# Streaming stage of a decoder step: scores in four quarters of the array, a third bank for transposes, a new order for the block choice

## The chip, the cores and the metric

One core of one Trainium2 chip runs the whole program as one launch. The metric is the device time of one execution in microseconds. Three executions of the kernel before were timed; the median counts.

## The reference, cut to what matters

One inference step of a decoder layer: 512 prompt tokens and 8 sequences with one new token each share the weights (width 1024, float32). The change lies in the attention of the 8 sequences. Each has 8 query heads of 64 in 2 groups, 1024 cached positions and a memory of 256 rows, and four kinds of scores against its own keys:

```python
# per sequence b, head h; one query token each
s_c = q @ kc.T          # 63 compressed blocks: kc = gelu(rows(32 tokens) @ w1) @ w2 + ...
imp = sum_heads(softmax(s_c)) for 17 blocks of 64 tokens; 16 are kept (the first and the last two always)
s_s = q @ k_sel.T       # 1024 cached keys and the new one, only in the chosen blocks
s_w = q @ k_win.T       # a window: 511 cached keys and the new one
s_m = qm @ k_mem.T      # 4 memory heads over 256 rows
o = g0 * softmax(s_c) @ vc + g1 * softmax(s_s) @ v_sel + g2 * softmax(s_w) @ v_win ;  o_mem = softmax(s_m) @ v_mem
```

Keys lie in memory by rows and must be turned (transposed on TensorE) before they can be multiplied.

## The kernel before

The program has stages: projection and streaming in one block (to about 305 us), then the prompt's attention and mixing, the routing, and 32 experts whose weights stream from memory up to the end. Each stage starts behind a barrier of all engines. The change touches only `stream()`.

**Streaming.** `ORDER` is 0, 1, 8, 2, 3, ..., 7; 8 stands for the prompt (its compression alone). A sequence comes in two halves of 512 cached rows. SyncE loads half i into one of four landing slots (`load_half`, L542; its waits are in `half_free`, L626: half i - 4 sorted, its values copied, its selection keys turned). GpSimd copies the compression rows of a half into one of two sorted buffers (`take_kv`, L803) and the selection values away (`take_vs`, L809). TensorE turns a sequence in 8 units of four 128 x 128 transposes (`turn`, L922): units 0 to 3 are compression rows (L933), 4 and 5 selection keys straight from the landing slot (L937), 6 window keys (L941), 7 memory keys (L945). Unit 4 is thus the one that frees a sequence's first half for the load of the half four further on. Units alternate between PSUM banks 4 and 5; ScalarE copies the even ones out (L871), VectorE the odd ones (L659). A unit waits until the copy of the unit two before is done (L926).

**Scores** (`score`, L979) of the sequence before are put between the first units of the next, in four parts: part 0 is the selection keys' first half and the window keys, 512 columns each with 64 stationary columns, one in the array's lower half (bank 0, partitions 0 to 63), one in the upper (bank 2, partitions 64 to 127); part 1 the selection keys' second half (bank 1); part 2 the memory keys (two products of 256 columns, 32 stationary columns, bank 3); part 3 the new keys (two of one column). `Q` holds 64 columns for each sequence, of which only its own 8 are not zero, so all sequences add up in the same 64 partitions.

**Compression** (`compress`, L958): 16 taps each for keys and values follow each three entries of `ORDER`, so the sequences come in three groups: (0, 1, prompt), (2, 3, 4), (5, 6, 7). Between the taps and their second product stands gelu, on VectorE (L666 to L673) with a tanh on ScalarE (L878); gelu stands in both engines' lists ahead of the copies of the next sequences.

**The end.** After the last keys' taps: VectorE copies the memory scores out of PSUM and takes their maximum, the same for the window, `keep_k(2)`, then the compressed scores (L741); ScalarE takes the exponents of memory, window, compressed (L894, L897, L900). TensorE sums the heads' probabilities (L1049, "the choice's product"), VectorE finds the block that falls out (L750 to L756), adds the mask while copying the selection scores out of PSUM (L761), takes the maximum over 1025 columns (L707), ScalarE the exponents (L903), then VectorE scales the window's and the choice's weights (L716). TensorE transposes the window's, memory's and compressed weights (L1054 to L1058), waits, transposes the choice's (L1065), and does all value products (L1074 to L1095) with 8 stationary columns in four quarters of the array. The last taps of the values' compression are spread over the waits. The output rows are gathered last (L1107).

## Time and profile before

| what | us |
|---|---|
| median of 3 runs | 1017.05 |
| runs | 1017.04 to 1019.19 |
| the profiled execution's own time | 1020.41 |
| its span, first to last instruction | 1018.6 |
| TensorE busy | 896.5 (88%) |
| VectorE, ScalarE, GpSimd busy | 315.2, 195.0, 124.2 |

In the rows further down, PE is TensorE, PEld its weight loads, DVE VectorE, ACT ScalarE, POOL GpSimd, SPq SyncE's queue. A row of a timeline is a run of equal instructions: start, duration until the end of the last, engine, line, operation, what it writes and reads, shape and count; in brackets the idle time of the engine before it and who ended it. A float32 product of the scores counts as two records. Ends of matmuls are modelled, so for TensorE the distance from start to start says more than a duration. PEclk is the clock that was granted to TensorE, as a share of 2.4 GHz.

### The profile page before, as it was taken

The numbers are of one execution on the slowest core, as the hardware profiler recorded it, in microseconds if no ns is written. First come the engines' busy times: TensorE is split into PE (matmuls) and PEld (weight loads), VectorE is DVE, ScalarE is ACT, GpSimd is POOL, SyncE is SP. The second block draws the span as 40 slices with busy tenths as digits, with TensorE's granted clock in tenths as the row PEclk, the third lists the DMA queues.
The fourth block names the chain that finished last, engine by engine and source line by source line (L and its number), as shares of the span: only waits on it lengthen the run. The fifth ranks groups of instructions, "written<-read, shape, count | busy, mean of one in ns | idle before, by whom it ended". The sixth has DMA issues, their size and how long they took to land.

```text
span 1018.6 us, 13659 instructions
## 1 busy us (share of the span) xinstructions
PE 896.5 (88%) x5483; PEld 500.1 (49%) x5483; DVE 315.2 (31%) x685; ACT 195.0 (19%) x468; POOL 124.2 (12%) x143
## 2 busy tenths in 40 slices
PE   7999989998988889989998999889788787787887
PEld 3445445564554446656555555445443444344443
DVE  3162242313335786564552111111111111111110
ACT  1031121202115675561110000001000000000000
POOL 0010023212000011120001111111111111111001
PEclk9999999999988899999997999999999999999999
DMA  9773127677208000005978999999999999999996
GB/s 363 322 237 102 57 75 172 137 174 180 90 2 299 1 1 2 1 1 216 384 291 320 416 415 415 411 417 413 412 420 415 410 417 408 416 412 414 416 410 224
DMA packets 66472, 272.12 MB, mean 267 GB/s; under 512 B 12048, under 2 KB 28367, under 8 KB 40991
## 3 DMA queue, kind: packets, MB, share of 16 engines
q1 hardware_dynamic: 52359, 254.17, 63.9%
q0 software_dynamic: 7376, 12.85, 4.6%
q10 hardware_dynamic: 6672, 4.20, 1.8%
q8 instruction: 45, 0.74, 0.3%
q14 instruction: 20, 0.16, 0.1%
HBM read 264.63 MB, written 19.10 MB: 279 GB/s over the span
## 4 chain that ended last, share of the span: by engine, by line
DMA 24%; PE 24%; SPq 12%; DVE 3%; ACT 3%; issue 3%; POOL 1%; POOLq 0%; DVEq 0%; ACTq 0%
DMA room<-in_w_gate 9%; SPq L2200 9%; PE ps L2340 6%; SPq L2204 4%; DMA spare<-in_w_up 3%; DMA w_b<-in_w_up 3%; PE ps L1905 3%; DMA room<-in_w_up 3%; DMA w_b<-in_w_down 3%; PE ps L1479 3%; DMA w_a<-in_w_up 3%; PE ps L2367 2%; PE ps L1387 1%; ACT w_a L1732 1%; PE ps L1405 1%
## 5 line engine op out<-in xcount | busy, mean ns | idle before, releaser
L2340 PE MATMUL ps<-room 128*64 128x256 f32 x800 | 98.2, 394 | 30.3 <-DMA room<-in_w_up 17.9
L2340 PEld LDWEIGHTS ps<-room 128*64 128x64 f32 x800 | 57.3, 140 | 67.4 <-DMA room<-in_w_up 26.0
L2254 POOL DMA_INDIRECT out_y<-room,halves x32 | 50.1, 1565 | 279.9 <-ACT room L2520 276.3
L2340 PE MATMUL ps<-w_a,room 128*64 128x256 f32 x576 | 69.3, 390 | 16.6 <-DMA w_a<-in_w_up 8.8
L2340 PE MATMUL ps<-w_b,room 128*64 128x256 f32 x576 | 67.7, 383 | 16.1 <-DMA w_b<-in_w_up 9.7
L505 PE MATMUL ps<-w_b,room 128*128 128x454 f32 x192 | 75.3, 544 | 1.0 <-ACT w_a L437 1.0
L2520 ACT ACTIVATE room<-ps,slot_w 128x512 f32<-128x512 f32 x32 | 22.0, 687 | 277.6 <-PE ps L2367 273.3
L972 PE MATMUL ps<-room,w_a 128*128 128x378 f32 x192 | 62.5, 483 | 0.0
L2340 PEld LDWEIGHTS ps<-w_a,room 128*64 128x64 f32 x576 | 40.9, 139 | 42.4 <-DMA w_a<-in_w_up 13.3
L2431 DVE SCALAR_TENSOR_TENSOR room<-room,ps 128x256 f32<-128x256 f32 x32 | 13.5, 422 | 152.3 <-ACT room L2514 152.3
L2340 PEld LDWEIGHTS ps<-w_b,room 128*64 128x64 f32 x576 | 40.0, 137 | 41.1 <-DMA w_b<-in_w_up 15.3
L2433 DVE TENSOR_TENSOR room<-room,ps 128x256 f32<-128x256 f32 x32 | 13.5, 421 | 133.7 <-PE ps L2340 133.7
L505 PEld LDWEIGHTS ps<-w_b,room 128*128 128x128 f32 x192 | 36.2, 190 | 37.4 <-issue 37.4
L2367 PE MATMUL ps<-room,consts 128*64 128x512 f32 x208 | 47.8, 599 | 0.5 <-DVE consts L2437 0.5
L972 PEld LDWEIGHTS ps<-room,w_a 128*128 128x128 f32 x192 | 36.0, 190 | 22.8
L2437 DVE COPY consts<-ps 128x256 f32<-128x256 f32 x32 | 13.6, 425 | 107.4 <-PE ps L2324 107.4
L2514 ACT ACTIVATE room<-ps 128x256 f32<-128x256 f32 x32 | 12.3, 383 | 170.8 <-PE ps L2340 170.8
L1732 ACT ACTIVATE w_a<-ps,room 128x256 f32<-128x256 f32 (+3 forms) x80 | 40.2, 514 | 12.7 <-DVE room L1579 12.6
L2208 POOL DMA_INDIRECT xg<-hn_dram,pairs x16 | 16.9, 1059 | 200.7 <-PE ps L2354 130.7
L659 DVE COPY room<-ps 128x512 f32<-128x512 f32 x33 | 22.8, 691 | 52.5 <-PE ps L933 39.9
L1479 PE MATMUL ps<-w_b,room 128*128 128x256 f32 x128 | 31.4, 401 | 3.5 <-POOL room L1339 2.0
L2367 PE MATMUL ps<-w_b,consts 128*64 128x512 f32 x144 | 33.1, 599 | 0.7 <-DMA w_b<-in_w_down 0.7
(376 smaller groups left out, 1221.0 us busy)
## 6 DMA issues: line engine op xcount, KB each, us to landing
room<-in_w_down SPq DMA_DIRECT2D x26, 1024.0 KB, 28.1
room<-in_w_gate SPq DMA_DIRECT2D x25, 1024.0 KB, 28.4
room<-in_w_up SPq DMA_DIRECT2D x25, 1024.0 KB, 28.3
w_a<-in_w_gate SPq DMA_DIRECT2D x18, 1024.0 KB, 27.0
w_a<-in_w_up SPq DMA_DIRECT2D x18, 1024.0 KB, 27.9
w_a<-in_w_down SPq DMA_DIRECT2D x18, 1024.0 KB, 28.4
w_b<-in_w_gate SPq DMA_DIRECT2D x18, 1024.0 KB, 28.3
w_b<-in_w_up SPq DMA_DIRECT2D x18, 1024.0 KB, 27.6
```

The lines of the kernel that those rows point to most:

```text
L505: ins = nc.tensor.matmul(in_psum(t, a), turned_rows(t)[:, k, 0:r], rhs, start=(k == 0), stop=(k == KD - 1))
L659: nc.vector.tensor_copy(dst, src).then_inc(out_d, 1)
L972: ins = nc.tensor.matmul(ps[:, 6 + q, 0:NG3], w1[:, q, l, :], XT[q][:, :, :, l % 8, l // 8:l // 8 + NC_S].rearrange("p s g m -> p (s g) m" ...
L1479: ins = nc.tensor.matmul(ps[:, 7, half:2 * half], mT[:, k, t * P:t * P + P], self.w_out[:, k, half * c:half * c + half], start=(k == 0), s ...
L1732: ins = nc.scalar.activation(pr[:, i // n, i % n, :], sc[:, i // n, i % n, :], ACT.Exp, bias=stt[:, u % 6, 0, i:i + 1], scale=-1.0, accum_ ...
L1905: ins = nc.tensor.matmul(ps[0:r, b + a, :], m[:, k, :], w_out[:, k, 512 * a:512 * a + 512], start=(k == 0), stop=(k == KD - 1))
L2200: sp.dma_start(self.gate_or_up(u, j), src[:, 4 * j:4 * j + 4, :]).then_inc(self.unit_in[j][u % RING], 16)
L2204: sp.dma_start(self.down_half(u, j), src[:, j, :, :]).then_inc(self.unit_in[j][u % RING], 16)
L2254: pool.indirect_dma_start(out=rows, out_offset=bass.IndirectOffsetOnAxis(ap=self.halves[:, n:n + 1].bitcast(U32), axis=0), in_=yb[:, slot, ...
L2340: ins = nc.tensor.matmul(ps[h * CAP:h * CAP + CAP, bank, 0:FH], xT[:, n // 2 % 2, k, CAP * slot:CAP * slot + CAP], w[k // 4][:, k % 4, h * ...
L2367: ins = nc.tensor.matmul(ps[a * CAP:a * CAP + CAP, 6 + n % 2, :], hT[:, j, h * CAP:h * CAP + CAP], wd[h][:, j, 512 * a:512 * a + 512], sta ...
L2520: nc.scalar.activation(yb[:, n % 2, :], ps[0:2 * CAP, 6 + n % 2, :], ACT.Copy, scale=self.slot_w[:, n:n + 1]).then_inc(y_copied, 1)
```

## The change

- Scores: a sequence's products are cut to the 32 columns that hold its own 8, and its four score sets go to four quarters of one bank: selection keys' halves to partitions 0 to 31 and 32 to 63, window keys to 64 to 95, memory keys to 96 to 127. Sequences 0 to 3 use bank 0, 4 to 7 bank 1. All five products are issued together, behind unit 1 of the next sequence; the new keys' part stays behind unit 3.
- Bank 2 is free for it: from the ninth unit on, turns go round banks 4, 5, 2, and wait for the copy of the unit three before.
- ScalarE copies the window's and the selection's scores from the quarters to 64 partitions in SBUF (six copies); VectorE copies only the memory's and the small ones.
- The choice: VectorE takes each block's maximum over the unmasked scores beforehand (16 numbers a row), adds the mask to these 16 and takes the maximum over 17, instead of over 1025; the mask's addition works in SBUF. `keep_k(2)` moves behind the window's maximum. The window's weights are scaled ahead of the choice.
- The compressed scores use two quarters. The choice's product comes after three more taps instead of four.
- TensorE does the window's value products ahead of the choice's transposes, which it did after them before.

```diff
+        win_taken, sel_taken = S("win_taken"), S("sel_taken")
...
-        sel0, win0, misc, hid, cmp_ = ps[:, 0:2, :], ps[:, 2, :], ps[:, 3, :], ps[:, 6, :], ps[:, 7, :]
+        win0, misc, hid, cmp_ = ps[:, 2, :], ps[:, 3, :], ps[:, 6, :], ps[:, 7, :]
...
         place = {s: j for j, s in enumerate(ORDER)}
...
+        early = units[ORDER[0]]
+        bank_of = [4 + n % 2 if n < early else (4, 5, 2)[(n - early) % 3] for n in range(NUNIT)]
+        earlier = [max((m for m in range(n) if bank_of[m] == bank_of[n]), default=None) for n in range(NUNIT)]
...
+        tops = late[0:64, 4000:4017]
...
                 for u in range(1, units[s], 2):
...
+                    src = ps[:, bank_of[first[s] + u], :]
...
-                        src = ps[:, 5, :].rearrange("p (g m r) -> p g r m", g=G, r=8)
+                        src = src.rearrange("p (g m r) -> p g r m", g=G, r=8)
...
-                        src = ps[:, 5, :]
...
-            ch.then(nc.vector.tensor_copy(smb[:, :], misc[64:96, 128:384]))
+            ch.then(nc.vector.tensor_copy(smb[:, :], ps[96:128, 0, 0:MEM]))
             peak(1, 32, smb[:, :], "mmax")
...
-            nc.vector.tensor_copy(swb[:, 1:512], win0[64:128, 1:512])
+            nc.vector.tensor_copy(ssb[:, 1024:1025], misc[0:64, 64:65])
...
+            dve.wait_ge(win_taken, 2)
+            peak(2, 64, swb[:, 1:513], "wmax")
             keep_k(2)
-            peak(2, 64, swb[:, 1:513], "wmax")
-            dve.wait_ge(cs_in_psum, 1)
+            dve.wait_ge(sel_taken, 4)
+            ch.then(nc.vector.tensor_reduce(tops[:, 0:2 * PAST // PAGE].rearrange("p (c k) -> p c k", c=4),
+                                            ssb[:, 0:PAST].rearrange("p (c t k j) -> p c k t j", c=4, t=2, k=4), AX.XY, ALU.max))
+            dve.wait_ge(cs_in_psum, 2)
...
             weights(0, 64, scb[:, 0:NC_S], None, "pc")
...
+            weights(2, 64, swb[:, 1:513], g64[:, 2:3], None)
+            ch.then(nc.vector.tensor_scalar(dgn[:, 1, :], self.c(C_ID, 64, 64), swb[:, 512:513], None, ALU.mult))
+            marks["wp"] = ch.n
             dve.wait_ge(imp_in_psum, 1)
...
+            ch.then(nc.vector.tensor_tensor(tops[:, 0:16], tops[:, 0:16], imp[:, 2, :], ALU.add))
+            nc.vector.tensor_copy(tops[:, 16:17], ssb[:, 1024:1025])
...
-                out4 = ssb[:, 0:1024].rearrange("p (c t k j) -> p c t k j", c=4, t=2, k=4)
-                in4 = sel0[0:64, :, :].rearrange("p a (c t k j) -> p (a c) t k j", c=2, t=2, k=4)
+                out4 = ssb[:, 0:1024].rearrange("p (c t k j) -> p c t k j", c=4, t=2, k=4)[:, :, par, :, :]
...
-                nc.vector.tensor_tensor(out4[:, :, par, :, :], in4[:, :, par, :, :], mask, ALU.add)
-            ch.then(nc.vector.tensor_copy(ssb[:, 1024:1025], misc[0:64, 64:65]))
-            peak(3, 64, ssb[:, 0:1025], "smax")
...
-            dve.wait_ge(es, 2)
-            weights(2, 64, swb[:, 1:513], g64[:, 2:3], None)
-            ch.then(nc.vector.tensor_scalar(dgn[:, 1, :], self.c(C_ID, 64, 64), swb[:, 512:513], None, ALU.mult))
-            marks["wp"] = ch.n
+                ins = nc.vector.tensor_tensor(out4, out4, mask, ALU.add)
+            ch.then(ins)
+            peak(3, 64, tops[:, 0:17], "smax")
...
                 for u in range(0, units[s], 2):
...
+                    src = ps[:, bank_of[first[s] + u], :]
...
-                        src = ps[:, 4, :].rearrange("p (g m r) -> p g r m", g=G, r=8)
+                        src = src.rearrange("p (g m r) -> p g r m", g=G, r=8)
...
-                        dst, src = KsT[:, 0:512] if u == 4 else KwT[:, :], ps[:, 4, :]
+                        dst = KsT[:, 0:512] if u == 4 else KwT[:, :]
...
             tanh(2, 0)
+            act.wait_ge(scored, NB)
+            for g in range(2):
+                nc.scalar.copy(swb[32 * g:32 * g + 32, 1:512], ps[64:96, g, 1:512]).then_inc(win_taken, 1)
             act.wait_ge(steps_d, marks["mmax"])
...
+            for g in range(2):
+                for hf in range(2):
+                    nc.scalar.copy(ssb[32 * g:32 * g + 32, 512 * hf:512 * hf + 512], ps[32 * hf:32 * hf + 32, g, :]).then_inc(sel_taken, 1)
             act.wait_ge(steps_d, marks["wmax"])
...
             def turn(s, u):
...
-                if n >= 2:
-                    pe.wait_ge(out_d if n % 2 else out_a, n // 2)
-                dst = ps[:, 4 + n % 2, :]
+                if earlier[n] is not None:
+                    pe.wait_ge(out_d if earlier[n] % 2 else out_a, earlier[n] // 2 + 1)
+                dst = ps[:, bank_of[n], :]
...
             def score(s, part):
-                q = Q[:, 64 * s:64 * s + 64]
-                if part == 0:
+                g = s // 4
+                q = Q[:, 64 * s + 32 * g:64 * s + 32 * g + 32]
+                if part == 1:
...
-                    nc.tensor.matmul(sel0[0:64, 0, :], q, KsT[:, 0:512], **add)
-                    nc.tensor.matmul(win0[64:128, :], q, KwT[:, :], **add)
-                elif part == 1:
-                    nc.tensor.matmul(sel0[0:64, 1, :], q, KsT[:, 512:1024], **add)
-                elif part == 2:
+                    nc.tensor.matmul(ps[0:32, g, :], q, KsT[:, 0:512], **add)
+                    nc.tensor.matmul(ps[32:64, g, :], q, KsT[:, 512:1024], **add)
+                    nc.tensor.matmul(ps[64:96, g, :], q, KwT[:, :], **add)
...
-                        nc.tensor.matmul(misc[64:96, 128:384], Qm[:, a, 32 * s:32 * s + 32], KmT[:, a, :], **add)
-                else:
+                        nc.tensor.matmul(ps[96:128, 0, 0:MEM], Qm[:, a, 32 * s:32 * s + 32], KmT[:, a, :], **add)
+                elif part == 3:
...
-                        ins = nc.tensor.matmul(misc[0:64, 64 + a:65 + a], q, kTn[:, a, s:s + 1], **add)
+                        ins = nc.tensor.matmul(misc[32 * g:32 * g + 32, 64 + a:65 + a], q, kTn[:, a, s:s + 1], **add)
...
                         score(before, u)
...
-                    score(before, 2)
...
-                    for a in range(4):
+                    for a in (0, 1, 3):
...
             compress(2, 0, range(16))
-            for part in range(4):
-                score(NB - 1, part)
+            score(NB - 1, 1)
+            score(NB - 1, 3)
...
             compress(2, 1, range(4, 6))
...
-            for b in range(NB):
-                ins = nc.tensor.matmul(misc[0:64, 0:NC_S], Q[:, 64 * b:64 * b + 64], kcT[:, place[b], 0:NC_S], start=False, stop=False, skip_group_check=True)
-            ins.then_inc(cs_in_psum, 1)
-            compress(2, 1, range(6, 10))
+            for i in range(4):
+                for g in range(2):
+                    b = 4 * g + i
+                    ins = nc.tensor.matmul(misc[32 * g:32 * g + 32, 0:NC_S], Q[:, 64 * b + 32 * g:64 * b + 32 * g + 32], kcT[:, place[b], 0:NC_S], **add)
+                    if i == 3:
+                        ins.then_inc(cs_in_psum, 1)
+            compress(2, 1, range(6, 9))
...
-            compress(2, 1, range(10, 16))
...
-            pe.wait_ge(steps_d, marks["wp"])
+            compress(2, 1, range(9, 16))
...
+            pe.wait_ge(steps_d, marks["cg"])
...
             pe.wait_ge(zeroed, 7)
             nc.tensor.matmul(win0, zb2[0:1, 0:128], zb2[0:1, :], start=True, stop=False, skip_group_check=True)
+            pe.wait_ge(sel_taken, 4)
...
-            pe.wait_ge(steps_d, marks["sp"])
-            for j in range(8):
-                nc.tensor.transpose(ps[:, 4, 64 * j:64 * j + 64], ssb[:, 128 * j:128 * j + 128], ident(64))
-            nc.tensor.matmul(hid[0:NB, 256:320], self.c(C_S8, NB, 64), dgn[:, 0, :], start=True, stop=True).then_inc(pT_in_psum, 1)
...
+            pe.wait_ge(steps_d, marks["sp"])
+            for j in range(8):
+                nc.tensor.transpose(ps[:, 4, 64 * j:64 * j + 64], ssb[:, 128 * j:128 * j + 128], ident(64))
+            nc.tensor.matmul(hid[0:NB, 256:320], self.c(C_S8, NB, 64), dgn[:, 0, :], start=True, stop=True).then_inc(pT_in_psum, 1)
```

## Rows read from the trace of the kernel before

**Rows 1.** Busy time by stage: us, length, busy of each engine (x instructions), PEclk, DMA share, GB/s.
```profile
139.00:163.00 24.00, 19.79 (x112) 11.52 (x110) 11.11 (x34) 7.61 (x14) 13.37 (x26) 0.93 0.62 151
...
183.50:208.00 24.50, 22.48 (x141) 13.56 (x140) 11.07 (x19) 7.27 (x13) 6.85 (x12) 1.00 0.82 184
...
228.30:257.20 28.90, 25.90 (x156) 14.66 (x155) 10.91 (x18) 7.30 (x13) 6.91 (x12) 1.00 0.66 167
...
287.40:294.20 6.80, 6.80 (x108) 3.74 (x106) 1.69 (x4) 1.20 (x3) 0.00 (x0) 0.51 0.01 2
```

**Rows 2.** TensorE in order of time, sequence 5: start us, us, engine line op, xcount.
```profile
228.87 0.64 PE L987 MATMUL ps<-room 128*64 128x512 f32 x1
...
229.88 0.66 PE L933 MATMUL ps<-consts,xg 128*128 128x128 f32 x4
230.47 1.07 PE L990 MATMUL ps<-room 128*64 128x512 f32 x2
...
232.05 1.05 PE L993 MATMUL ps<-room 128*32 128x256 f32 x4
...
233.62 0.39 PE L996 MATMUL ps<-room 128*64 128x1 f32 x4
233.94 1.19 PE L937 MATMUL ps<-consts,w_a 128*128 128x128 f32 x8
235.27 0.66 PE L941 MATMUL ps<-consts,room 128*128 128x128 f32 x4
```

**Rows 3.** GpSimd in order of time, copies out of the landing buffer.
```profile
201.79 1.17 POOL L803 COPY xg<-w_a 128x512 f32<-128x512 f32 x2 [2.75 <-DMA w_a<-in_cache_kv]
...
246.40 1.17 POOL L803 COPY xg<-w_a 128x512 f32<-128x512 f32 x2 [10.85 <-DMA w_a<-in_cache_kv]
...
250.95 1.17 POOL L803 COPY xg<-w_a 128x512 f32<-128x512 f32 x2 [2.82 <-DMA w_a<-in_cache_kv]
```

**Rows 4.** TensorE in order of time, first transposes of late half-sequences.
```profile
203.10 0.63 PE L933 MATMUL ps<-consts,xg 128*128 128x128 f32 x4 [0.39 <-POOL xg L803]
...
252.27 0.63 PE L933 MATMUL ps<-consts,xg 128*128 128x128 f32 x4 [1.32 <-POOL xg L803]
```

**Rows 5.** All engines in order of time, 267 to 287 us.
```profile
270.31 0.55 DVE L673 SCALAR_TENSOR_TENSOR room<-spare,room 128x378 f32<-128x378 f32 x1 [0.58 <-ACT spare L878]
...
277.17 0.35 ACT L900 ACTIVATE room<-room 64x63 f32<-64x63 f32 x1 [1.05 <-DVE room L708]
...
279.06 0.33 PE L1049 MATMUL ps<-room,consts 64*64 64x64 f32 x2
...
280.96 1.28 DVE L761 TENSOR_TENSOR w_a<-ps,room 64x512 f32<-64x512 f32 x2
...
283.77 1.15 ACT L903 ACTIVATE w_a<-w_a,room 64x1025 f32<-64x1025 f32 x1 [6.16 <-DVE room L708]
...
286.45 0.71 PE L1065 MATMUL ps<-consts,w_a 64*128 64x64 f32 x8
```

**Rows 6.** TensorE in order of time, products with the values in quarters.
```profile
291.64 3.12 PE L1080 MATMUL ps<-w_a 128*4 128x256 f32 x32
...
295.23 1.93 PE L1088 MATMUL ps<-w_b,w_a 128*8 128x128 f32 x64
```

**Rows 7.** Groups by line, 139 to 305 us: xcount, busy us, mean ns, idle before.
```profile
L659 DVE COPY room<-ps 128x512 f32<-128x512 f32 x33 | 22.8, 691 | 52.5 <-PE ps L933 39.9 <-PE ps L937 6.5 <-PE ps L945 6.1
...
L871 ACT COPY room<-ps 128x512 f32<-128x512 f32 x33 | 19.2, 583 | 57.4 <-PE ps L933 37.4 <-PE ps L937 13.4 <-PE ps L941 6.5
```

**Rows 8.** All engines in order of time, 239 to 240 us.
```profile
239.84 0.57 ACT L871 COPY room<-ps 128x512 f32<-128x512 f32 x1
```

**Rows 9.** TensorE in order of time, the first group of sequences.
```profile
144.06 2.11 PE L937 MATMUL ps<-consts,w_a 128*128 128x128 f32 x8
...
153.23 0.63 PE L933 MATMUL ps<-consts,xg 128*128 128x128 f32 x4 [0.50 <-POOL xg L803]
...
163.08 20.27 PE L972 MATMUL ps<-room,w_a 128*128 128x378 f32 x63
```

## The prediction

> **What bounds the kernel now.** I first read the busy time by stage [rows 1]. The change touches one stage, the streaming of the eight cached sequences, from about 139 to 305 us. In its three groups of sequences (139 to 163, 183.5 to 208 and 228.3 to 257.2 us) TensorE is busy for 19.8 of 24, 22.5 of 24.5 and 25.9 of 28.9 us; between the groups it runs the compression taps, which the change leaves alone. Every other engine is busy for under 60% of any group. So TensorE's list of work sets the pace, with gaps. The DMA share of 0.82 and 0.66 says that the loads come close behind.
>
> Then the list itself [rows 2]. In sequence 5 a unit of four transposes takes 0.59 us when nothing holds it (229.88 to 230.47). Between the first four units stand the scores of the sequence before: 1.01 us (228.87 to 229.88, two products of 512 columns side by side in halves), 1.00 (one in a half), 0.99 (memory keys), and 0.32 (new keys, 233.62 to 233.94): 3.3 us. Two units in a row take 1.33 us instead of 1.18: with two banks a unit waits for the copy of the one two before.
>
> Third, the loads [rows 3]: GpSimd takes sequence 7's two halves at 246.40 and 250.95 only because they landed then (10.85 and 2.82 us of idle before), and sequence 4's second at 201.79. TensorE waits for these copies [rows 4]: 0.39 us at 203.10, 1.32 us at 252.27. These two places matter most: a faster TensorE arrives early there.
>
> Last, the end of the stage [rows 5]: the gelu of the last compression ends at 270.86; the exponents of the compressed scores start at 277.17, the block choice's product at 279.06, the mask's two additions (1.28 us) at 280.96, the choice's exponents (1.15 us) at 283.77, their transposes at 286.45. From there TensorE works to the end of the stage nearly without a gap. The next stage starts behind a barrier, so what the stage gains should pass on whole. Later stages are not changed.
>
> **The scores in quarters.** Five products (three of 512 columns, two of 256 into one quarter) replace those that took 3.0 us; the 0.32 us part stays. Do four quarters overlap? Value products do it already [rows 6]: 32 products of 128 columns in 1.93 us are 60 ns each, where half a score of 512 columns alone takes 1.0 us, or 250 ns per 128. That is four at once. The 256-column ones (16 in 3.12 us, mostly at half clock [rows 1]) agree. None has 512 columns, so I bound the set by 1.0 (perfect) and 2.0 us (pairs only) and take 1.1, nearest to those rows. Gain: 1.9 us for each score on the path.
>
> **The third bank.** A unit then waits for the copy of three before. A copy takes 0.691 us on VectorE and 0.583 on ScalarE [rows 7], each engine taking every second unit (1.18 us apart), so this hides: 0.15 us saved per pair, some 0.3 to 0.35 per sequence. It doesn't hide where gelu lies ahead of the copies: ScalarE's copy of sequence 6's first unit begins at 239.84 [rows 8], 3.3 us after the last unit of sequence 5. With units 0 to 2 and a score in 2.9 us, unit 3 then waits about 1 us. The load hides that in groups 2 and 3.
>
> **Group 1** [rows 9]. Sequence 1's second half comes from GpSimd at about 153.1 us (TensorE's unit at 153.23), held by the gate's chain and not by TensorE. The score ahead of it costs nothing either way. Behind it the 0.99 us part and the bank waits go: sequence 1 ends 1.2 us earlier. The next score (before the taps at 163.08) saves 1.9 and two bank or copy waits 0.4. Sum 3.5 us.
>
> **Group 2.** Sequence 4's load starts when sequence 2's fifth unit is turned. No score lies ahead of it there, so relative to the group's start that comes only 0.3 us earlier. DMA carries this load at its rate (share 0.82 over the group [rows 1]), so its second half is ready at 202.96 less 0.3. What lies behind shrinks from 4.9 us (203.10 to 208.0) to six units, the 0.32 and nothing else: 3.6. Gain 0.3 + 1.3 = 1.6 us, while TensorE alone would have offered 4.8 (two scores and three sequences' bank waits): it now waits some 2.6 us before this half.
>
> **Group 3.** Here the score of sequence 4 lies ahead of the fifth unit: the load starts 1.8 us earlier. Behind its second half again 4.9 becomes 3.6 (252.27 to 257.2). Gain 3.1 us. The waits before the two halves of sequence 7 grow to some 2.6 and 2.2 us.
>
> Sum by the last compression's taps: 3.5 + 1.6 + 3.1 = 8.2 us.
>
> **The end of the stage** [rows 5], counted from the end of those taps (267.4 before). The last score is 1.9 us shorter, but VectorE starts on the softmaxes only once the gelu is done, at +3.5 in both kernels: nothing. ScalarE gets six copies more. Two (window) run while VectorE does the gelu's last step and cost nothing: without that cover 1.2 us. The memory exponents start at +4.5 and end at +5.2, then four copies at 0.58 [rows 7] until +7.5; VectorE waits for them with the compressed scores queued behind, then takes the blocks' maxima (1024 columns, like the two additions of 1.28 us): +8.9. Compressed exponents at +9.5 against +9.8 (277.17). Their normalisation takes 1.0, so the choice's product starts at +10.5. Before, it stood at +11.7 behind four taps; now three taps and shorter compressed scores leave TensorE free at +9, with 1.5 us of wait. From that product to the choice's exponents it was 4.7 us. The window's weights (1.0 us) come ahead of it, 0.65 of them uncovered; the 1.2 us maximum over 1025 columns becomes 17 columns (0.17). Sum 4.35: exponents at +14.85 against +16.35. Meanwhile TensorE does the remaining seven taps, the window's transposes and the zeroing (to +17.0), waits for ScalarE's copies behind the exponents, and starts the value products at +17.4. Before, the equal amount of work started at +19.05 (286.45). Gain 1.6 us.
>
> **Sum and clock.** 8.2 + 1.6 = 9.8 us. Against this stands TensorE's clock. The granted clock was 0.51, the 1.2 GHz level, from 287.4 to 294.2 us [rows 1], behind a wait and small products; and two units that take 1.19 us took 2.11 at 144.06 [rows 9] behind a wait of 2.7 us for ScalarE. The change makes three or four waits of that size. A stretch at half clock costs up to half its length where TensorE is the bound (3.4 us for 6.8), and nothing where it waits. I bound it by 0 and 5 us and take 1.7. The stretch near the end may also vanish, which would give up to 3.4 back. Forecast: 8.1 us off.
>
> The profiled execution took 1020.41 us for a span of 1018.6; so the sum gives 1012.3 for it. The runs' median is 1017.05; by the same difference 1008.9, which I give as 1009.0.
>
> **Rivals.** (a) *The copies become the bound.* If each unit waits for a copy (0.69 + 0.1 us) instead of taking 0.59, six units behind each late half and in group 1 take 1.2 us more: 9.8 - 3.6 - 1.7 = 4.5 us off, 1012.5. Against it: each copying engine is busy under half of a group [rows 1]. The Trainium skill (TensorEngine Tiling (Array Packing), section Performance Considerations) says that after a fourfold speedup the copying out of PSUM may become the bottleneck; by that rule the result would be this one. Chance 0.08.
> (b) *Slower: the clock.* Place: the waits before sequences 4's and 7's halves, in group 1, and before the choice's product. If each of the four is followed by 6.8 us at half clock under dense taps, that is 4 x 3.4 = 13.6 us against 9.8: 1017.05 + 3.8 = 1020.9. It decides once more than 19.6 us at half clock fall on bound work. For it: the two stretches above. Against: most of such a stretch would fall on the wait itself, and taps before and after are dense. The Trainium skill (TensorE: Matmul & The Clock Gate, section HAM oscillation) describes this: waits for DMA between bursts make each burst start cold. By that rule the time would lie towards this rival. Chance 0.03; a partial form (5 us off, 1012) 0.12.
> (c) *Quarters overlap only in pairs*: 0.9 us more for the three scores on the path: 5.4 us off, 1011.7. The value products speak against it. Chance 0.06.
> (d) *The half-clock stretch at the end goes*: 11.5 us off, 1005.5. Chance 0.1.
> (e) *The loads follow TensorE less or more than I think* (something other than the fifth unit starts them): at worst groups 2 and 3 gain only the 1.3 each behind the half: 3.5 + 2.6 + 1.6 less 1.7 is 6.0 us off, 1011.0. Chance 0.06.
> The rest, 0.55, is the forecast.
>
> **How the numbers follow.** Outside 1004.5 to 1013.0 lie (b) in full, parts of (d) and of the partial clock case: under 2 in 10. A measurement of this kernel can tell about 0.2% (2 us) from no change. Faster by more: 0.95. Within: 0.02. Slower: 0.03.
>
> **What would show it.** A sequence's five score products in about 1.1 us; units 0.59 us apart; GpSimd's copies of sequence 7's halves still waiting for DMA, with TensorE waiting over 2 us for each; taps starting 3.5, 5.1 and 8.2 us earlier; the choice's exponents about 15 us after the last compression's taps of the first kind. The forecast is wrong if TensorE doesn't wait for GpSimd at sequence 7 (then more is gained), if ScalarE's four copies end later than 7.5 us after those taps, or if half-clock stretches grow by over 5 us.

## The result, and the profile after

| what | kernel before | changed kernel |
|---|---|---|
| median, us | 1019.27 (10 runs, 1017.04 to 1024.91) | 1011.04 (10 runs, 1008.01 to 1013.75) |
| the profiled execution's own time, its span | 1020.41, 1018.6 | 1012.05, 1010.2 |
| TensorE busy | 896.5 | 874.9 |

The ratio is 0.9907, with a 95% interval of 0.988 to 0.9933: the changed kernel is faster, by 8.2 us between the medians, which is under 1%. The forecast was a gain of 8.1 us, to 1009.0. The changed kernel's median lies 2.0 us above that because the kernel before came out 2.2 us higher over ten runs than over the three that the forecast started from. So the size of the gain was right, but in part by luck: in this pair of traces the edits were worth some 12.5 us where 9.8 were forecast, and the clock cost some 4.2 us where 1.7 were taken (worked out below).

First the busy time by stage, as in [rows 1], of the changed kernel: the three groups of sequences, 14 us of the end, and the stretch that had half the clock in group 3.

```profile
139.90:158.80 18.90, 13.01 (x113) 9.68 (x111) 11.32 (x34) 7.65 (x14) 9.60 (x19) 1.00 0.58 152
179.20:204.20 25.00, 17.93 (x142) 14.83 (x141) 11.07 (x19) 7.04 (x13) 8.58 (x15) 0.86 0.87 202
224.50:249.00 24.50, 18.68 (x156) 14.34 (x155) 10.91 (x18) 7.12 (x13) 6.91 (x12) 0.93 0.78 192
241.30:244.50 3.20, 2.97 (x17) 2.12 (x18) 0.69 (x1) 0.59 (x1) 0.64 (x2) 0.50 1.15 269
278.00:292.00 14.00, 12.13 (x302) 9.51 (x290) 3.12 (x6) 2.04 (x5) 0.00 (x0) 1.00 0.01 2
```

The reader is to see that TensorE's busy time fell in each group (19.8, 22.5 and 25.9 before), that groups 1 and 3 are shorter and group 2 is not, and that its clock was granted in full at the end, where before it was 0.51 for 6.8 us.

Then TensorE's list in sequence 5, which answers to [rows 2]. The numbers behind the columns are those of the rows before.

```profile
225.44 0.62 PE L1005 MATMUL ps<-room 128*32 128x512 f32 x1
225.44 0.62 PE L1006 MATMUL ps<-room 128*32 128x512 f32 x1
225.45 0.62 PE L1007 MATMUL ps<-room 128*32 128x512 f32 x1
225.46 0.62 PE L1009 MATMUL ps<-room 128*32 128x256 f32 x2
225.89 0.59 PE L1005 MATMUL ps<-room 128*32 128x512 f32 x1
...
226.44 1.09 PE L950 MATMUL ps<-consts,xg 128*128 128x128 f32 x8
227.46 0.29 PE L1012 MATMUL ps<-room 128*32 128x1 f32 x4
227.68 1.09 PE L954 MATMUL ps<-consts,w_a 128*128 128x128 f32 x8
228.60 0.60 PE L958 MATMUL ps<-consts,room 128*128 128x128 f32 x4
229.04 0.62 PE L962 MATMUL ps<-consts,room 128*128 128x128 f32 x4
```

All four quarters begin their first pass within 0.02 us and their second 0.45 us later; the next unit follows 1.00 us after the first. And a unit now takes 0.44 to 0.46 us from start to start (227.68 to 228.60 for two, then 229.04), where the forecast had 0.59.

Third, TensorE's waits for GpSimd's copies of the late halves, in TensorE's own list, answering to [rows 4], with what comes behind them:

```profile
192.72 1.06 PE L950 MATMUL ps<-consts,xg 128*128 128x128 f32 x8 [1.40 <-POOL xg L813]
...
198.93 1.94 PE L950 MATMUL ps<-consts,xg 128*128 128x128 f32 x8 [4.15 <-POOL xg L813]
...
201.10 1.97 PE L954 MATMUL ps<-consts,w_a 128*128 128x128 f32 x8
...
204.15 20.49 PE L989 MATMUL ps<-room,w_a 128*128 128x378 f32 x64
...
241.53 1.94 PE L950 MATMUL ps<-consts,xg 128*128 128x128 f32 x8 [3.71 <-POOL xg L813]
...
245.85 1.06 PE L950 MATMUL ps<-consts,xg 128*128 128x128 f32 x8 [0.79 <-POOL xg L813]
```

and the copies themselves in GpSimd's list, answering to [rows 3]:

```profile
191.40 1.17 POOL L813 COPY xg<-w_a 128x512 f32<-128x512 f32 x2 [7.69 <-DMA w_a<-in_cache_kv]
...
197.61 1.17 POOL L813 COPY xg<-w_a 128x512 f32<-128x512 f32 x2 [4.48 <-DMA w_a<-in_cache_kv]
...
240.22 1.17 POOL L813 COPY xg<-w_a 128x512 f32<-128x512 f32 x2 [10.83 <-DMA w_a<-in_cache_kv]
...
244.53 1.17 POOL L813 COPY xg<-w_a 128x512 f32<-128x512 f32 x2 [2.59 <-DMA w_a<-in_cache_kv]
```

TensorE's waits in groups 2 and 3 for these copies were 1.7 us in all at the two places of [rows 4], and 2.4 with the 0.67 us ahead of sequence 7's first half; at four places they are 10.05 now. Sequence 4's halves land 6.2 us apart (4.5 before), sequence 7's 4.3. Two transposed units take 1.94 us at half the clock in place of 1.06.

Last the end of the stage, all engines in order of time, answering to [rows 5]:

```profile
266.71 1.21 DVE L748 TENSOR_REDUCE w_a<-w_a 64x16 f32<-64x1024 f32 x1 [1.44 <-ACT w_a L912]
...
268.63 0.35 ACT L917 ACTIVATE room<-room 64x63 f32<-64x63 f32 x1 [1.11 <-DVE room L714]
...
269.68 0.33 PE L1067 MATMUL ps<-room,consts 64*64 64x64 f32 x2 [1.62 <-DVE room L720]
...
274.11 1.15 ACT L920 ACTIVATE w_a<-w_a,room 64x1025 f32<-64x1025 f32 x1 [5.04 <-DVE room L714]
...
276.53 0.62 PE L1089 MATMUL ps<-room,w_a 8*8 8x128 f32 x16 [0.32 <-ACT w_a L927]
```

**Where the time went.** The table cuts each profiled execution the same way, always at the starts of TensorE's work: the stage from its first transposes to the next stage's; the groups from there, or from the end of the taps before, up to the keys' taps (the taps between the groups take 20.3 to 20.4 us each, and more only in the last four rows); the end from the start of the last keys' taps; and the rest behind the stage. "Half clock" is the time in groups 1, 2, 3 and the end at which the granted clock was about 0.5, the 1.2 GHz level. x4 is the kernel before once more, and the other names are those of the experiments.

| kernel | stage | group 1 | group 2 | group 3 | end | half clock | rest |
|---|---|---|---|---|---|---|---|
| before | 166.4 | 24.3 | 24.5 | 28.8 | 48.0 | 3.4, 0, 0, 6.8 | 713.4 |
| x4, before again | 164.5 | 23.6 | 24.3 | 28.2 | 47.8 | 0, 0, 0, 6.8 | 719.7 |
| changed | 152.3 | 18.9 | 25.0 | 24.4 | 43.2 | 0, 6.8, 3.4, 0 | 718.1 |
| x1, two banks | 158.3 | 21.9 | 24.7 | 27.7 | 43.2 | 6.8, 6.8, 3.4, 0 | 718.1 |
| x2, products apart | 158.7 | 22.2 | 23.2 | 29.4 | 43.2 | 0, 0, 0, 0 | 712.3 |
| x3, keys later | 152.4 | 18.9 | 22.7 | 25.3 | 44.8 | 0, 3.4, 6.8, 3.4 | 715.4 |
| x5, choice first | 157.5 | 21.3 | 25.9 | 24.5 | 45.1 | 6.8, 10.2, 3.4, 3.4 | 712.2 |
| x6, max over 1025 | 154.3 | 18.9 | 25.5 | 25.3 | 43.9 | 0, 6.8, 6.8, 3.4 | 713.4 |
| x7, both back | 155.0 | 18.9 | 25.3 | 25.6 | 44.5 | 0, 6.8, 6.8, 3.4 | 712.4 |
| y1, units 4 and 5 early | 141.7 | 18.9 | 16.9 | 18.5 | 43.2 | 0, 0, 3.4, 0 | 712.5 |
| z, before with y1's edit | 161.6 | 24.3 | 22.6 | 22.4 | 46.4 | 3.4, 0, 0, 3.4 | 719.9 |
| y3, y1 and max over 1025 | 146.4 | 21.8 | 18.4 | 18.4 | 44.0 | 10.2, 3.4, 3.4, 3.4 | 716.8 |
| y4, y3 and gelu later | 140.7 | 21.3 | 15.9 | 15.9 | 43.9 | 6.8, 0, 0, 3.4 | 711.9 |

The stage became 14.1 us shorter in this pair (12.2 against x4), and 4.7 us of it are not in the total because the stages behind took that much longer, in a part of the program that the change doesn't touch. Two windows of each show it, the kernel before first (the attention of the prompt, then the mixing):

```profile
305.20:479.00 173.80, 155.29 (x999) 98.44 (x999) 112.45 (x243) 98.05 (x283) 16.91 (x19) 0.94 0.20 74
479.00:546.40 67.40, 60.78 (x307) 36.19 (x307) 34.78 (x92) 8.22 (x17) 2.19 (x2) 0.92 0.83 333
```

and the changed kernel:

```profile
292.20:468.60 176.40, 157.65 (x998) 100.34 (x998) 112.88 (x243) 97.96 (x283) 16.91 (x19) 0.92 0.19 73
468.60:538.60 70.00, 63.51 (x306) 38.36 (x306) 34.87 (x92) 8.11 (x17) 2.20 (x2) 0.88 0.82 323
```

The work of VectorE and ScalarE is the same, TensorE's takes 5.1 us longer in all, and its mean clock is lower (0.92 and 0.88 against 0.94 and 0.92). Over both stages that is 44.2 us at half clock against 30.6.

### The profile page after: what moved, and what is told of

Same layout as the page of the kernel before. It is cut to its first block, busy times and chain, and to the rows that moved or that the text cites. A ratio compares the mean times of both kernels' runs of the same rounds, so it can differ in the third digit from the quotient of the medians.

```text
span 1010.2 us, 13665 instructions
## 1 busy us (share of the span) xinstructions
PE 874.9 (87%) x5482; PEld 499.7 (49%) x5482; DVE 315.6 (31%) x687; ACT 197.9 (20%) x474; POOL 123.8 (12%) x143
## 4 chain that ended last, share of the span: by engine, by line
PE 30%; DMA 18%; SPq 14%; DVE 3%; issue 3%; ACT 2%; POOL 1%; POOLq 0%; DVEq 0%; ACTq 0%
SPq L2219 10%; PE ps L2359 9%; DMA w_b<-in_w_up 8%; SPq L2223 4%; PE ps L2386 4%; PE ps L1498 3%; PE ps L1924 3%; DMA w_b<-in_w_down 3%; DMA w_b<-in_w_gate 3%; DMA room<-in_w_up 3%; PE ps L1406 1%; PE ps L1424 1%; PE ps L1452 1%; ACT w_a L1751 1%; PE ps L2373 1%
## 5 line engine op out<-in xcount | busy, mean ns | idle before, releaser
L2359 PE MATMUL ps<-w_a,room 128*64 128x256 f32 x576 | 69.2, 390 | 18.1 <-DMA w_a<-in_w_up 9.7
L2386 PE MATMUL ps<-room,consts 128*64 128x512 f32 x208 | 47.8, 598 | 0.5 <-DVE consts L2456 0.5
L2456 DVE COPY consts<-ps 128x256 f32<-128x256 f32 x32 | 13.6, 424 | 107.4 <-PE ps L2343 107.4
L1751 ACT ACTIVATE w_a<-ps,room 128x256 f32<-128x256 f32 (+3 forms) x80 | 40.2, 515 | 10.2 <-DVE room L1598 10.1
L950 PE MATMUL ps<-consts,xg 128*128 128x128 f32 x136 | 20.5, 296 | 18.1 <-POOL xg L813 12.2
## 6 DMA issues: line engine op xcount, KB each, us to landing
w_a<-in_w_up SPq DMA_DIRECT2D x18, 1024.0 KB, 27.7
w_a<-in_w_down SPq DMA_DIRECT2D x18, 1024.0 KB, 28.2
w_b<-in_w_gate SPq DMA_DIRECT2D x18, 1024.0 KB, 27.7
```

Of the source, the lines that this page charges most:

```text
L1751: ins = nc.scalar.activation(pr[:, i // n, i % n, :], sc[:, i // n, i % n, :], ACT.Exp, bias=stt[:, u % 6, 0, i:i + 1], scale=-1.0, accum_ ...
L2359: ins = nc.tensor.matmul(ps[h * CAP:h * CAP + CAP, bank, 0:FH], xT[:, n // 2 % 2, k, CAP * slot:CAP * slot + CAP], w[k // 4][:, k % 4, h * ...
L2386: ins = nc.tensor.matmul(ps[a * CAP:a * CAP + CAP, 6 + n % 2, :], hT[:, j, h * CAP:h * CAP + CAP], wd[h][:, j, 512 * a:512 * a + 512], sta ...
```

## Experiments

All edits are against the changed kernel, unless it says otherwise. Each ratio is to the kernel before, timed beside it on the same chip.

**Without the third bank.**

```diff
-        bank_of = [4 + n % 2 if n < early else (4, 5, 2)[(n - early) % 3] for n in range(NUNIT)]
+        bank_of = [4 + n % 2 for n in range(NUNIT)]
```

> The changed kernel, but its turns use banks 4 and 5 alone, as before. Measure: from the first turn of sequence 0 to the first transposes of the next stage (166.4 us before, 152.3 after the change), and the starts of the three groups of taps. If the third bank is worth what the prediction gives it (0.3 us a sequence, on the path in group 1 and behind the late halves): group 1 grows by 0.7 us, groups 2 and 3 by 0.3 to 0.5 us each, the stage by 1.3 to 1.7 us. Rival: the changed trace has units 0.45 us apart in rows of three and more, against 0.66 with two banks, so that the bank is worth 0.2 us for every unit on the path: group 1 grows by about 1.8 us, groups 2 and 3 by 1.2 us or more each, the stage by 4 to 5 us (without stretches at half clock).

Measured: 1012.11 us (4 runs), ratio 0.9874 (0.9827 to 0.992). The interval overlaps the changed kernel's (0.988 to 0.9933), so the total shows no loss. The trace does: group 1 is 3.0 us longer, group 3 3.3, the stage 6.0. Of this up to 3.4 us is clock, since 6.8 us more lie at half clock. Group 2 is 0.3 us shorter by a side effect: sequence 5's keys are loaded only at 195.79, when the first half is there, and the second half follows 4.4 us behind it (x3, below, shows what these loads do). Three units of sequence 5, at full clock, stand 0.65 us apart, not 0.44:

```profile
229.47 1.20 PE L954 MATMUL ps<-consts,w_a 128*128 128x128 f32 x8
230.80 0.66 PE L958 MATMUL ps<-consts,room 128*128 128x128 f32 x4
231.45 0.66 PE L962 MATMUL ps<-consts,room 128*128 128x128 f32 x4
```

From 227.68 to 229.04 the changed kernel does three units, in 1.36 us; here they take 1.98. That is 0.6 us for three units, against the forecast's 0.15 per pair. In group 2 units wait 0.24, 0.21 and 1.64 us for copies, and for the halves of sequence 7 it still waits 3.03 and 2.35.

**The products apart again**, one part behind each unit, in quarters all the same.

```diff
-                if part == 1:
+                if part == 0:
...
                     nc.tensor.matmul(ps[0:32, g, :], q, KsT[:, 0:512], **add)
+                elif part == 1:
                     nc.tensor.matmul(ps[32:64, g, :], q, KsT[:, 512:1024], **add)
+                elif part == 2:
                     nc.tensor.matmul(ps[64:96, g, :], q, KwT[:, :], **add)
...
+                    score(before, 2)
                     score(before, 3)
```

> The changed kernel, with the score products of a sequence not together but one behind each of the next sequence's first four units, so that nothing overlaps; same quarters, same banks, same end. TensorE's work grows by 3.2 us a sequence (4 x 1.0 + 0.3 against 1.05 + 0.3). If the loads limit groups 2 and 3 as predicted: group 1 grows by 6 us (two scores on the path), group 2 by under 2 us (the score products fill the wait for the late half), group 3 by 4 to 6 us (the load starts 3.2 us later, and 1.3 us more lies behind the late half). Rival, that TensorE's list alone sets all three: each group grows by 6.4 us and more (two scores each), about 19 us in all.

Measured: 1016.18 us (10 runs), ratio 0.9951 (0.9922 to 0.9979): by the ratios about half of the gain is lost, but the interval just touches the changed kernel's, and that of the kernel before timed once more (0.9943 to 0.9993, below) too. The trace is clearer. The stage is 6.4 us longer than in the changed kernel. TensorE's list in sequence 5 shows why; each product alone takes as long as the set of four (0.98 us from 226.36 to 227.34):

```profile
226.36 1.04 PE L1005 MATMUL ps<-room 128*32 128x512 f32 x2
227.34 0.66 PE L950 MATMUL ps<-consts,xg 128*128 128x128 f32 x4
227.92 1.04 PE L1007 MATMUL ps<-room 128*32 128x512 f32 x2
...
200.58 0.63 PE L950 MATMUL ps<-consts,xg 128*128 128x128 f32 x4 [1.20 <-POOL xg L813]
...
246.02 0.63 PE L950 MATMUL ps<-consts,xg 128*128 128x128 f32 x4 [2.02 <-POOL xg L813]
```

Group 1 loses 3.3 us, not the expected 6: only one of its two scores is on the path, the other stands ahead of a wait for GpSimd. Group 3 loses 5.0. But group 2 is 1.9 us shorter than in the changed kernel: sequence 5's keys are loaded at 194.72, as the first half lands, so that the second half is copied 16.9 us into the group in place of 18.5; TensorE's wait for it is 1.20 us in place of 4.15; and no stretch of a group lies at half clock. So what packing the products saves in group 2 is worth nothing there as long as the loads stay where they are. The rival, 6.4 us and more in each group, is out.

**Sequence 5's window and memory keys loaded later**, with sequence 6's (ScalarE's queue).

```diff
-                if s + 2 < NB:
+                for t in {3: (), 4: (5, 6)}.get(s, (s + 2,) if s + 2 < NB else ()):
                     act.wait_ge(turned, first[s] + 8)
-                    self.load_new_keys(act, s + 2)
+                    self.load_new_keys(act, t)
```

> The changed kernel, with ScalarE's loads of sequence 5's window and memory keys issued one sequence later (behind sequence 4 instead of 3). In the changed trace sequence 4's second half is taken by GpSimd 6.2 us after its first, where it was 4.5 us before the change; those key loads are issued in between. If they delay the half: the distance falls to 4.4 to 4.6 us, TensorE's wait there from 4.2 to about 2.5 us, and the stretch at half clock that began in this wait may go; group 2 gets 1.7 us shorter, or up to 4 us with the clock. Rival, that the half is late because of SyncE's own queue or the DMA rate: the distance stays at 6.2 us and group 2 at 25.0 us.

Measured: 1009.57 us (4 runs), ratio 0.9864 (0.9824 to 0.9905). In the changed kernel ScalarE's queue issues two loads of keys while sequence 4's halves are on their way:

```profile
189.87 0.55 ACTq L561 DMA_DIRECT2D room<-in_cache_win  x1
190.45 0.82 ACTq L562 DMA_DIRECT2D room<-in_cache_mem  x1
```

Without these two, GpSimd's list of this experiment is

```profile
191.91 1.17 POOL L813 COPY xg<-w_a 128x512 f32<-128x512 f32 x2 [7.83 <-DMA w_a<-in_cache_kv]
...
196.29 1.17 POOL L813 COPY xg<-w_a 128x512 f32<-128x512 f32 x2 [2.66 <-DMA w_a<-in_cache_kv]
```

4.4 us apart in place of 6.2. TensorE's second wait falls from 4.15 to 2.32 us and group 2 from 25.0 to 22.7. Before the change the same two loads were issued when the first half had landed, and the halves stood 4.5 us apart:

```profile
197.31 1.17 POOL L803 COPY xg<-w_a 128x512 f32<-128x512 f32 x2 [9.25 <-DMA w_a<-in_cache_kv]
...
198.09 0.55 ACTq L561 DMA_DIRECT2D room<-in_cache_win  x1
...
198.67 0.65 ACTq L562 DMA_DIRECT2D room<-in_cache_mem  x1
```

The other traces agree. Where the two loads go out 1.5 us or more ahead of the first half's copy (changed kernel, x5, x6, x7) the halves are copied 6.2 to 6.7 us apart; where they go out 0.2 us ahead of it or later (before, x4, x1, x2) 4.4 to 4.5. The gain in the total is within the intervals, and the stage of this execution is no shorter (152.4 us): group 3 and the end have 6.8 us more at half clock.

**The kernel before, once more**, as a null.

> The kernel before once more, for a second profile. In the first pair of profiles the streaming stage got 14.1 us shorter, but all behind it took 4.6 us more (718.1 against 713.4 us), with 13.6 us more at half clock in the two stages that follow. If that is chance (where the stretches at half clock fall in an execution): this profile's rest lies between 713 and 719 us, and over all profiles of the study rest and half-clock time go together and don't hang on the stage ahead. Rival, that the shorter stage causes it (another position or a colder start): this one lies within 1 us of 713.4 and all the profiles with the short stage at 717 and more. The streaming stage itself: 166.4 us, less 3.4 us or so if it has no half-clock stretch near its end.

Measured: 1018.52 us (10 runs), ratio 0.9968 (0.9943 to 0.9993). So a ratio can be 0.3% off without a cause. Its rest behind the stage is 719.7 us in the trace: 6.3 us more than in the first profile of the same program, and a little above the range that was expected.

**The order of the choice's transposes back** (ahead of the window's value products), **the maximum over 1025 columns back**, and **both**. In x5 the block of eight transposes from `pe.wait_ge(steps_d, marks["sp"])` on stands ahead of the value products again. In x6:

```diff
-            dve.wait_ge(sel_taken, 4)
-            ch.then(nc.vector.tensor_reduce(tops[:, 0:2 * PAST // PAGE].rearrange("p (c k) -> p c k", c=4),
-                                            ssb[:, 0:PAST].rearrange("p (c t k j) -> p c k t j", c=4, t=2, k=4), AX.XY, ALU.max))
...
-            ch.then(nc.vector.tensor_tensor(tops[:, 0:16], tops[:, 0:16], imp[:, 2, :], ALU.add))
-            nc.vector.tensor_copy(tops[:, 16:17], ssb[:, 1024:1025])
+            dve.wait_ge(sel_taken, 4)
...
-            peak(3, 64, tops[:, 0:17], "smax")
+            peak(3, 64, ssb[:, 0:1025], "smax")
```

> The changed kernel, but TensorE again transposes the choice's weights ahead of all value products, as before the change. Measure: from the start of the last keys' taps to the next stage's first transposes: 43.24 us in the changed kernel, the same in two other runs without half clock there; 47.97 and 47.76 before, each with 6.8 us at half clock. In the changed trace the choice's weights are ready at 276.74 us and the first value products start at 276.53, so they could hardly have started sooner with the old order: 43.5 us (0.2 to 0.4 more). Rival: the new order is what shortened the end; then 1.5 us and more come back, and with TensorE idle and on small products longer, the stretch at half clock with its 3 us too: 45 to 48 us.

> The changed kernel without the block maxima taken ahead: VectorE adds the mask and takes the maximum over 1025 columns as before the change. If the maxima ahead shorten the chain as the change intends, the choice's exponents come 0.8 us later after the mask is known (1.2 us against 0.17, 0.17 and 0.15). Rival, and what I expect from the changed trace: the 1.21 us that the block maxima take stand ahead of the compressed scores on VectorE, in the same chain; without them the compressed exponents come 1.1 us sooner, and the choice's exponents in sum 0.3 us sooner than in the changed kernel (14.97 us after the last keys' taps there). The end (43.24 us): 42.9 to 43.1 by the rival, 43.6 to 44.0 by the first, if value products wait for it at all.

> Both of the last two edits undone together. If the order of TensorE's products hides the choice's chain (each alone cheap, since the window's products cover 2.5 us of a late choice), both together cost more than their sum. If the chain isn't longer with the old maximum (the rival above), the two together cost what the order alone costs: 43.2 to 43.5 us. Otherwise 44.3 us and more.

Measured, one execution each: 1010.18, 1009.08 and 1009.0 us. That tells nothing between them, so the traces have to. The order alone moves TensorE's first work of the value phase from 17.4 to 17.65 us behind the end of the last keys' taps: 0.26 us. The block maxima lengthen the chain. With x6's edit the taps end at 260.18, and

```profile
269.48 0.32 PE L1063 MATMUL ps<-room,consts 64*64 64x64 f32 x2 [0.38 <-DVE room L720]
...
276.78 0.62 PE L1085 MATMUL ps<-room,w_a 8*8 8x128 f32 x16 [0.78 <-ACT w_a L923]
```

put the choice's product at +9.3 (changed kernel: +10.5) and the first value products at +16.6 (+17.4). The 1.21 us of maxima stand ahead of the compressed scores on VectorE and make TensorE wait 1.62 us; 1025 columns later cost less than that. With both back the value phase begins at +17.2, where the changed kernel has +17.4: the two edits together bring nothing in the chain.

The length of the end says something else. It is 43.2 us in the changed kernel and 43.9 in x6, inside the range that x6's expectation gave to the other theory. The value products start 0.8 us sooner, but from there to the next stage x6 takes 17.06 us and the changed kernel 15.60, with 3.4 us at half clock (0.50) in x6 and none in the changed kernel. All four kernels without the block maxima (x6, x7, y3, y4) have such a stretch there; of the five with the maxima and with the window's products first (the changed kernel, x1, x2, x3, y1) only x3 has it, and its end is 44.8 us. x5 has it too (45.1 us, expected 43.5), and x7 (44.5, expected 43.2 to 43.5). Whether the missing maxima bring the stretch or chance does is open. So the 0.8 us are a cost in the chain, but none of the four ends without the maxima is shorter than 43.9 us.

**Units 4 and 5 turned early.** From here on versions that try to beat both kernels. Sequences 2 and 5 open groups 2 and 3; their fifth unit starts the load that these groups wait for. It needs only the landing slot, so it can be turned between the keys' and the values' taps, with the score of the sequence before ahead of it. Units 4 and 5 then wait until GpSimd has sorted their half, which was a given before, and the copies out of PSUM follow the new order.

```diff
+        AHEAD = (ORDER[3], ORDER[6])
+        turns = {s: [4, 5, 0, 1, 2, 3, 6, 7] if s in AHEAD else list(range(units[s])) for s in ORDER}
...
-                    if before is not None:
+                    if before is not None and s not in AHEAD:
...
                     compress(j // 3, 0, range(16))
+                    if s != NB:
+                        score(s, 1)
+                        score(s, 3)
+                    for u in (4, 5):
+                        turn(ORDER[j + 1], u)
                     compress(j // 3, 1, range(16))
```

> The changed kernel with one thing moved: sequences 2 and 5 have their units 4 and 5 (selection keys straight from the landing slots) turned between the keys' and the values' taps ahead of them, so that the loads of sequences 4 and 7 start some 10 us earlier, under taps; the score of sequence 4 goes there too. By my theory (the loads of sequences 4 and 7 start with unit 4 of sequences 2 and 5 and set the pace of groups 2 and 3; the waits of 1.4, 4.2, 3.7 and 0.8 us and the half clock behind them are theirs): all four waits go, the groups take TensorE's own 17.5 and 19 us instead of 25.0 and 24.4, the streaming stage 139 to 142 us instead of 152.3, and the kernel 998 to 1001 us where the changed one takes 1011. Rival: the DMA rate (1 MB in 4.5 us) or GpSimd limits them, so that the waits only move to sequences 5 and 6: the stage stays at 148 us or more.

Measured: 996.11 us (6 runs), ratio 0.9774 (0.9738 to 0.9809). The stage is 141.7 us, group 2 16.9 and group 3 18.5, the rest 712.5. Part of each group's work now stands among the taps ahead of it; group and taps together are 7.2 and 3.4 us shorter than in the changed kernel. That is what the theory expected, and the rival (148 us or more) is out. In TensorE's list no wait of groups 2 and 3 for a late half is above 0.25 us:

```profile
187.87 0.66 PE L953 MATMUL ps<-consts,xg 128*128 128x128 f32 x4 [2.16 <-ACT room L885]
...
209.40 0.63 PE L958 MATMUL ps<-consts,w_a 128*128 128x128 f32 x4 [0.23 <-POOL xg L816]
...
227.62 0.66 PE L953 MATMUL ps<-consts,xg 128*128 128x128 f32 x4 [2.15 <-ACT room L885]
```

**The same with the kernel before**: halves, two banks, the old end, and only the early turns. The edit is that of the run above, with all four parts of the score ahead of the two turns.

> The kernel before (halves, two banks, the old end), with only the new order of turns: units 4 and 5 of sequences 2 and 5 are turned between the keys' and the values' taps, and the score of the sequence before them goes there too. Theory (before the change TensorE's own work sets the pace in the groups, so an earlier landing has little to give): its waits for GpSimd's late copies were only 0.39 and 1.32 us, so those go, 1 to 3 us off in all, ratio 0.997 to 0.999 to the kernel before. Rival (the loads bound the kernel before as much as the changed one): 15 us off as for the changed kernel, 0.985.

Measured: 1018.88 us (12 runs), ratio 0.9988 (0.9968 to 1.0008), no difference that can be told. The stage is 161.6 us, 2.9 less than x4's. The early turns are worth nothing measurable in the total without the change, and some 14 us with it (0.9907 less 0.9774, each against the kernel before timed beside it).

**Early turns with the old maximum**, and **with gelu one or two copies later on top of that**. The second edit, on VectorE (`k` picks the units of a sequence; `between` runs behind gelu's fourth step) and ScalarE:

```diff
-                gelu(j, 1)
-                out(b)
+                out(b, slice(1, 2))
+                gelu(j, 1, lambda: out(b, slice(3, 4)))
+                out(b, slice(5, None, 2))
...
-                tanh(j, 1)
-                out(b)
+                out(b, slice(0, 4, 2))
+                tanh(j, 1)
+                out(b, slice(4, None, 2))
```

> The changed kernel with the early turns, and the choice's maximum taken over 1025 columns again in place of the block maxima ahead of it. Theory (the block maxima stand on VectorE ahead of the compressed scores and cost 0.8 us at the value products): the choice's product 9.3 us behind the last keys' taps in place of 10.5, value products at +16.6 in place of +17.4, 0.8 us off the version with the early turns alone. Rival (the end hides it behind the zeroing and the window's work): no difference.

> The kernel of the run before this one in the list, with gelu and its tanh of the values' compression of groups 1 and 2 moved one copy later on VectorE and two copies later on ScalarE, and one copy put between gelu's parts on VectorE. Theory (the 2.15 us waits of TensorE for ScalarE's copy behind the tanh are the last ones in groups 2 and 3 and are bound work): both waits shrink below 0.7 us, each group 1.5 to 2 us shorter, 3 to 4 us off in all, if the loads still arrive in time. Rival (the loads are close behind again): TensorE waits for GpSimd's copies of the last halves by as much as is saved, under 1 us off.

Measured: 1002.02 us for the first (6 runs, 994.63 to 1006.08, ratio 0.9806, 0.9766 to 0.9846) and 993.89 for the second (6 runs, 990.24 to 996.42, ratio 0.9743, 0.9712 to 0.9775). The first's total shows none of the 0.8 us, since its executions spread over 11 us, with 10.2 us at half clock in group 1 of the profiled one. Its chain does: counted from the end of the last keys' taps (252.25) the choice's product is at +9.3 and the value products at +16.6, as in x6. The second is the fastest kernel of the study, 2.6% below the kernel before. The waits behind the tanh are 1.18 us in place of 2.16, in TensorE's list:

```profile
190.40 0.66 PE L961 MATMUL ps<-consts,room 128*128 128x128 f32 x4 [1.18 <-DVE room L668]
...
228.72 0.66 PE L961 MATMUL ps<-consts,room 128*128 128x128 f32 x4 [1.18 <-DVE room L668]
```

Expected were waits under 0.7 us and 3 to 4 us off; the waits shrank by 1.0 us each. That is 2 us off by the trace; the 8 us between the two medians are more than it explains, and the spread of the first is the likelier source of the rest. Against the early turns alone (0.9774, 0.9738 to 0.9809) the second's ratio isn't told apart.

## Why the prediction was right, and where not

**Scores in quarters: right.** Predicted 1.1 us a set between bounds of 1.0 and 2.0; it takes 1.00. Rival (c), pairs only, is out. Undoing it (x2) costs 6.4 us of the stage.

**The third bank: too small.** The forecast took "0.15 us saved per pair" from 0.59 us a unit. That 0.59 was a unit between score products; it holds something that isn't the four transposes. Units in a row take 0.44 to 0.46. So the bank saves 0.2 us a unit (x1) and not 0.07. This is the term that was mis-sized most: it stands behind the larger gains of groups 1 and 3.

**Group 1: mechanism right, size off.** Predicted 3.5 us, measured 5.5, or 4.7 against x4, which has no half-clock stretch there. The missing 1.2 is mostly the faster units: eight of them lie behind sequence 1's second half, each 0.13 us shorter than the forecast's 0.59.

**Group 2: wrong.** Predicted 1.6 us off, measured 0.5 longer. The step that failed is "its second half is ready at 202.96 less 0.3": counted from the group's start the load was issued 0.8 us sooner and not 0.3 (at +3.3, before +4.1), since the units ahead of it are faster, and the first half's copy came 1.6 us sooner (191.40 - 179.2 = 12.2, before 197.31 - 183.5 = 13.8), but the second at +18.5, before +18.3. Sequence 5's keys, which were loaded 14.6 us into the group, now go out at 10.7 us, ahead of both landings; x3 shows their cost by taking them away. The prediction weighed the loads' start and rate but not what else would be on the DMA engines at the new time. Then came the clock: behind that wait two units took 1.97 us and the stretch to the taps 5.2 (198.93 to 204.15), where group 3 has 3.0 (245.85 to 248.89) at full clock and the forecast 3.6. That is 2.2 us.

**Group 3: right in kind.** Predicted 3.1, measured 4.4. The stretch behind the last half is 3.0 us against 3.6, and the last landing came 2.6 us sooner, not 1.8 (GpSimd's copy of the last half is at +20.1 from the group's start at 224.47, before at +22.6). The waits were expected as 2.6 and 2.2 us and were 3.71 and 0.79: 4.5 in all against 4.8. The half clock there (241.2 to 244.6) ended in a wait for GpSimd that would have been longer without it, so it cost nothing.

**The end: right to 0.1 us in the chain.** Compressed exponents at +9.5 (predicted +9.5), choice's product +10.5 (+10.5) behind a wait of 1.62 (1.5), choice's exponents +15.0 (+14.85), value products +17.4 (+17.4). What the forecast lacked is that two of its edits cancel: it credited the maximum over 17 columns with 1.0 us behind the choice's product, while the cost of the block maxima lay hidden in its "+8.9" ahead of it. The forecast of the chain as a whole was right because both were in its sum.

**Clock: right in sign over the whole kernel, too small, and not where it was looked for.** Taken: 1.7 us lost. Inside the stage the pair of traces shows a gain: the change lost 2.2 us in group 2, and was spared 0.7 in group 1 (x4, without a half-clock stretch there, is that much shorter than the first profile) and 3.1 at the end (4.7 us shorter, 1.6 of it in the chain). So the stretch of rival (d), given 0.1, did go, but the rival's 11.5 us off didn't come, because more was lost elsewhere. The stretch at the end is in both profiles of the kernel before (6.8 us), absent in those of the changed kernel, x1, x2 and y1, and 3.4 us long in x3, x5, x6, x7, y3, y4 and z. By the Trainium skill (TensorE: Matmul & The Clock Gate, section HAM oscillation) bursts behind waits for DMA start cold; behind the 4.15 and 3.71 us waits they did, and behind x2's waits of 1.20 and 2.02 they did not, but neither did the one behind x1's wait of 3.03 us. The price stayed far under 13.6 us, and rival (b) is out.

**The rest behind the stage: not foreseen.** "What the stage gains should pass on whole" failed by 4.7 us in this pair. It doesn't hang on the length of the stage: the two shortest stages (141.7 us in y1 and 140.7 in the last kernel) have rests of 712.5 and 711.9, and the three profiles with the old scores have 713.4, 719.7 and 719.9. Across the profiles of this study the two stages behind take 239.5 to 248.3 us, with 27 to 48 us at half clock, about half a microsecond for each. So of the 14.1 us in the stage 12.5 are the edits' work and 1.6 the clock's; they met 4.7 us of this and a start of the stage 1.1 us later (behind 3.4 us at half clock near 65 us, which the first profile of the kernel before doesn't have), and came out at 8.4.

**Is the lower clock chance?** Not all of it. Each timed execution has its mean granted clock on record. It is 0.966 in the changed kernel's ten (0.962 to 0.969). On the chip of x1 to x4 it is 0.967 in the eight of x1 and x3, whose groups are nearly those of the changed kernel, but 0.972 in 29 of the kernel before (0.965 to 0.978). A difference of 0.005 over 1010 us is an estimated 10 us more at half clock and costs up to 5 us. So the change does lower the clock on average. Kernels with shorter waits in groups 2 and 3 have it mostly back: 0.973 (x2, ten executions), 0.971 (y1 and y4, six each), but y3 has 0.967 in six (0.961 to 0.976). That the waits are the cause is not shown, and most of the half clock of a profile lies in stages that no edit touched. What decides in one execution which stretches fall to half clock stays open.

**Rival (a), the copies as bound**: out in this kernel. The Trainium skill (TensorEngine Tiling (Array Packing), section Performance Considerations) warns of copying out of PSUM; the waits of units for copies that are left in groups 2 and 3 are 1.52 and 1.32 us, both behind gelu's tanh. Where two banks stay (x1), it is true in small: a unit takes 0.65 us, about half of what its transposes (0.6) and its copy (0.69 or 0.58) take one after the other in the same bank. **Rival (e)** happened in half: group 2 gained less than its 1.3, by the loads and by the clock behind its wait.

**What would show it.** Of the prediction's signs most came: the set of scores in 1.00 us, GpSimd's copies of sequence 7's halves waiting for DMA, the choice's exponents at +15.0, ScalarE's four copies ending at +7.5. Units 0.59 us apart did not (0.45), nor did two waits of over 2 us before sequence 7's halves (3.71 and 0.79). The taps of the three groups start 5.5, 5.0 and 9.4 us earlier, counted from the stage's start, where 3.5, 5.1 and 8.2 were expected. And one sign of being wrong came: half-clock stretches were not to grow by over 5 us, and in this pair of profiles they grew by 10.3 (58.9 to 69.2 in the whole span).
